# Trainium2 case: the convolution layer's first projection in plain f32 products from the loaded panels, one output tile a panel, with the depthwise convolution tile by tile

## The reference

```
u = rms_norm(h, norm_mix_pre)              # h: 272 x 2048
u = u @ w_in + b_in                        # w_in: 2048 x 4096
a, g = split(u, 2)
u = a * sigmoid(g)
u = causal depthwise convolution of u, 31 taps, + b_dw
u = silu(layer_norm(u, ln_g, ln_b))
u = u @ w_out + b_out
```

## Time and profile before

| quantity | before |
|---|---|
| median of three runs | 3382.66 us (3377.47 to 3384.52) |
| span of the profiled execution, first to last instruction | 3380.4 us |
| TensorE matmul busy | 2816.1 us (83%) |
| VectorE busy | 1935.4 us (57%) |
| ScalarE busy | 949.7 us (28%) |
| GpSimd busy | 944.8 us (28%) |
| mean granted TensorE clock | 0.937 |

### The profile page before, as it was taken

The page is one execution under the profiler, slowest core; times in us unless marked ns, Lnnn a source line. Parts: engine busy times, 40 slices in busy tenths (PEclk is TensorE's granted clock), DMA queues, the critical chain, the costliest instruction groups (busy, mean ns, idle before and its releaser), DMA issues.

```text
span 3380.4 us, 39590 instructions
## 1 busy us (share of the span) xinstructions
PE 2816.1 (83%) x14622; PEld 2102.8 (62%) x14622; DVE 1935.4 (57%) x2548; ACT 949.7 (28%) x1197; POOL 944.8 (28%) x621
## 2 busy tenths in 40 slices
PE   6766397999999997989999997777777787777777
PEld 6766276999999996979999794333333333332233
DVE  4999845555555555385444455555555555655553
ACT  5222235444444444334333342111111111111110
POOL 5777000000000000030000004554545554546452
PEclk9888698999999998899999999989999999899999
DMA  5322043555555553433455547999999999999998
GB/s 215 108 96 105 19 174 112 186 186 186 186 186 186 186 185 113 149 125 142 175 181 195 189 150 298 408 405 411 412 414 411 413 411 412 410 408 409 406 413 339
DMA packets 117532, 855.07 MB, mean 253 GB/s; under 512 B 13104, under 2 KB 13104, under 8 KB 13248
## 3 DMA queue, kind: packets, MB, share of 16 engines
q0 software_dynamic: 74656, 543.27, 39.2%
q1 hardware_dynamic: 42800, 310.85, 25.8%
HBM read 851.97 MB, written 2.10 MB: 253 GB/s over the span
## 4 chain that ended last, share of the span: by engine, by line
PE 44%; DMA 18%; DVE 18%; issue 11%; POOL 5%; ACT 3%; DVEq 0%; POOLq 0%; SPq 0%; ACTq 0%
DMA s_u<-in_expert_u,s_expert 18%; PE bank L1390 14%; PE bank L1392 14%; PE bank L1391 14%; DVE s_u L1319 6%; POOL s_u L466 2%; POOL s_v L473 2%; DVE s_cacc L946 2%; DVE s_w_lo L875 1%; DVE s_yrow L1039 1%; PE bank L1669 1%; DVE s_qrs L1077 1%; ACT s_w_hi L498 1%; POOL s_w_lo L408 1%; ACT s_xs L504 0%
## 5 line engine op out<-in xcount | busy, mean ns | idle before, releaser
L1669 PE MATMUL bank<-s_v,s_diag 128*128 128x512 f32 x2048 | 996.8, 638 | 308.7 <-ACT s_diag L838 178.6
L1390 PE MATMUL bank<-s_a_hi,s_w_hi 128*128 128x256 f32 (+1 forms) x3072 | 883.8, 288 | 104.5 <-POOL s_w_lo L408 80.5
L875 DVE TENSOR_TENSOR s_w_lo<-s_raw,s_w_hi 128x2048 fp32r<-128x2048 f32 x260 | 597.2, 2297 | 647.7 <-ACT s_w_hi L498 647.3
L1669 PEld LDWEIGHTS bank<-s_v,s_diag 128*128 128x128 f32 x2048 | 399.8, 203 | 905.6 <-issue 723.5
L1391 PE MATMUL bank<-s_a_lo,s_w_hi 128*128 128x256 f32 (+1 forms) x3072 | 880.7, 287 | 0.0
L1392 PE MATMUL bank<-s_a_hi,s_w_lo 128*128 128x256 f32 (+1 forms) x3072 | 880.2, 287 | 0.0
L1319 DVE CUSTOM_DVE_ANT_0 s_u<-s_u,s_xn 128x2048 f32<-128x2048 f32 x256 | 583.2, 2292 | 499.6 <-DMA s_u<-in_expert_u,s_expert 497.4
L498 ACT ACTIVATE s_w_hi<-s_raw 128x2048 fp32r<-128x2048 f32 x259 | 496.2, 1916 | 653.0 <-PE bank L1392 652.9
L1390 PEld LDWEIGHTS bank<-s_a_hi,s_w_hi 128*128 128x128 f32 x3072 | 593.7, 193 | 112.6 <-POOL s_w_lo L408 83.9
L1392 PEld LDWEIGHTS bank<-s_a_hi,s_w_lo 128*128 128x128 f32 x3072 | 593.8, 193 | 0.0
L1391 PEld LDWEIGHTS bank<-s_a_lo,s_w_hi 128*128 128x128 f32 x3072 | 590.5, 192 | 1.4 <-issue 1.0
(11 more groups left out here) (264 smaller groups left out, 2169.6 us busy)
## 6 DMA issues: line engine op xcount, KB each, us to landing
s_raw<-in_stream SPq DMA_DIRECT2D x292, 1024.0 KB, 4.8
s_u<-in_expert_u,s_expert POOLq DMA_INDIRECT x256, 15.3
s_v<-in_expert_v,s_expert POOLq DMA_INDIRECT x256, 16.4
s_xres<-in_x SPq DMA_DIRECT2D x2, 1024.0 KB, 6.6
out<-s_out_row SPq DMA_DIRECT2D x2, 1024.0 KB, 6.8
s_bout_row<-in_b_out POOLq DMA_DIRECT2D x1, 1024.0 KB, 8.9
s_gmix_row<-in_g_mix_post POOLq DMA_DIRECT2D x1, 1024.0 KB, 12.4
s_gffn_row<-in_g_ffn_post POOLq DMA_DIRECT2D x1, 1024.0 KB, 16.8
```

What stands on the lines that cost most here:

```text
L875: dve.tensor_tensor(w_lo[s % 2][:, :], raw[s][:, :], w_hi[s % 2][:, :].bitcast(f32), ALU.subtract)\
L1390: pe.matmul(dst, left[0], right[0], start=start, stop=False)
L1669: ins = pe.matmul(bank[4 * t + c][:, :], diag[s % NDIAG][:, :], v_slot[s % NV][:, c * 512:(c + 1) * 512], start=False, stop=False)
```

## The change

* **Weights.** The panels of the first projection are laid out anew (`laid_out`): a panel now holds all 16 input tiles for one output tile; for each pair of output tiles (`a` j, `g` j) there are two panels. There are still 32 panels of 1 MB.
* **Products.** TensorE multiplies straight from `s_raw` with unsplit f32 activations `s_a_f` (a new name for the room of `a_hi` and `a_lo`), 16 matmuls of 272 columns a panel into bank c, 512 matmuls of type f32 in place of 1536 of type f32r. ScalarE's split and GpSimd's subtraction of this stage are gone, and so are the semaphores `hi_half` and `conv_split`.
* **Convolution.** One tile at a time. Even taps add into `cacc[:, 0]`, odd taps into `cacc[:, 1]`, and a last tensor_tensor adds the two sums into `s_cvo`. Taps 0 and 1 are tensor_scalar instructions. ScalarE's sigmoid and VectorE's `glu` also go by single tiles.
* **Prologue.** A root on a constant loads ScalarE's table at the start. ScalarE scales the first 128 tokens and the meta tokens, VectorE the other 128. The eight banks are emptied once: three by ScalarE (`ACT_BANKS`), five by VectorE (`DVE_BANKS`, one instruction a bank), and the meta tokens by one VectorE instruction.
* **Behind.** The layer norm's sum waits for 15 tiles, then for the sixteenth (before 14 and 16). The split of the next projection's first panel follows the stage as before.

The core of the diff:

```diff
+ACT_BANKS = ((0, 3), (1, 1), (1, 3))
+DVE_BANKS = ((0, 0), (0, 1), (0, 2), (1, 0), (1, 2))
...
+    a_f = place("s_a_f", [128, KT, L], S - 2 * ((KT * L * 4 + 63) // 64 * 64))
...
-            with n.rounds(pool, "norm0"):
-                pass
-            with n.rounds(pool, "w_in", 4):
-                for c in range(8):
-                    s = c % 4
-                    for ready, key, half in ((hi_half, "hi_half", slice(0, 1024)), (hi_ready, "hi", slice(1024, 2048))):
-                        pool.wait_ge(ready, n.after(key, c if key == "hi" else c + 1))
-                        ins = pool.tensor_tensor(w_lo[s % 2][:, half], raw[s][:, half], w_hi[s % 2][:, half].bitcast(f32),
-                                                 ALU.subtract)
-                    ins.then_inc(conv_split, 1)
...
+                act.activation(stat[:, 7:8], stat[:, 7:8], ACT.Sqrt)
...
-                for t in range(TT):
-                    act.activation(xs0[:, t, :], xres[:, t, :], ACT.Copy, scale=stat[:, 4 + t:5 + t])\
-                        .then_inc(xs_ready, 1)
+                act.activation(xs0[:, 0, :], xres[:, 0, :], ACT.Copy, scale=stat[:, 4:5]).then_inc(xs_ready, 1)
                 act.activation(meta_sb[:, :], meta_sb[:, :], ACT.Copy, scale=stat[0:META, 6:7]).then_inc(xs_ready, 1)
-                act.wait_ge(raw_loaded[0], 16)
-                act.activation(w_hi[0][:, 0:1024], raw[0][:, 0:1024], ACT.Copy).then_inc(hi_half, 1)
-                act.activation(w_hi[0][:, 1024:], raw[0][:, 1024:], ACT.Copy).then_inc(hi_ready, 1)
                 act.wait_ge(cols_loaded, 16)
-                transposed_hi("g_mix", META)
-                act.wait_ge(panel_used, n.after("used", 1))
-                for k in range(KT):
-                    ins = act.activation(a_hi[:, k, 0:META], bank[0][:, k * META:(k + 1) * META], ACT.Copy,
-                                         scale=col("g_mix", k))
-                ins.then_inc(evac_hi, 1)
+                for t, b in ACT_BANKS:
+                    act.wait_ge(bank_full[4 * t + b], n.after(f"full{4 * t + b}", 1))
+                    for q in range(4):
+                        k = 4 * b + q
+                        ins = act.activation(a_f[:, k, META + t * 128:META + (t + 1) * 128],
+                                             bank[4 * t + b][:, q * 128:(q + 1) * 128], ACT.Copy, scale=col("g_mix", k))
+                    ins.then_inc(bank_empty[4 * t + b], 1)
 
 
             with n.rounds(act, "w_in", 4) as i:
-                for c in range(8):
-                    split_hi(c, halves=True)
-                    if c % 4 < 3:
-                        continue
-                    j = c // 4 * 2
-
-                    act.wait_ge(bank_empty[j + 1], n.after(f"empty{j + 1}", 0))
-                    act.wait_ge(bank_full[4 + j], n.after(f"full{4 + j}", 1))
-                    act.activation(sig[:, j, :], bank[4 + j][:, 0:L], ACT.Sigmoid,
-                                   bias=cols[:, bass.ds(i * 4 + (COL["b_g"] + j), 1)]).then_inc(bank_empty[4 + j], 1)
-                    j += 1
-                    act.wait_ge(panel_used, n.after("used", c + 1))
-                    act.activation(sig[:, j, :], bank[4 + j][:, 0:L], ACT.Sigmoid,
-                                   bias=cols[:, bass.ds(i * 4 + (COL["b_g"] + j), 1)]).then_inc(bank_empty[4 + j], 1)
+                for j in range(4):
+
+                    wait(act, bank_empty[2 * j], n.after(f"empty{2 * j}", 0))
+                    act.wait_ge(panel_used, n.after("used", 2 * j + 2))
+                    act.activation(sig[:, j, :], bank[2 * j + 1][:, 0:L], ACT.Sigmoid,
+                                   bias=cols[:, bass.ds(i * 4 + (COL["b_g"] + j), 1)]).then_inc(bank_empty[2 * j + 1], 1)
+            split_hi(-1)
...
+                dve.wait_ge(rstd_ready, n.after("rstd", 1))
+                dve.tensor_scalar(xs0[:, 1, :], xres[:, 1, :], stat[:, 5:6], None, ALU.mult).then_inc(xs_late_ready, 1)
                 dve.wait_ge(cols_loaded, 16)
-                transposed_lo("g_mix", META)
-                dve.wait_ge(evac_hi, n.after("evac", 9))
-                for k in range(KT):
-                    ins = dve.scalar_tensor_tensor(a_lo[:, k, 0:META], bank[0][:, k * META:(k + 1) * META], col("g_mix", k),
-                                                   a_hi[:, k, 0:META].bitcast(f32), ALU.mult, ALU.subtract)
-                ins.then_inc(bank_empty[0], 1)
+                for t, b in DVE_BANKS:
+                    dve.wait_ge(bank_full[4 * t + b], n.after(f"full{4 * t + b}", 1))
+                    gains = cols[:, COL["g_mix"] + 4 * b:COL["g_mix"] + 4 * b + 4].unsqueeze(2).to_broadcast([128, 4, 128])
+                    dve.tensor_tensor(a_f[:, 4 * b:4 * b + 4, META + t * 128:META + (t + 1) * 128], four_tiles(4 * t + b), gains,
+                                      ALU.mult).then_inc(bank_empty[4 * t + b], 1)
+                dve.wait_ge(panel_used, n.after("used", 1))
+                gains = cols[:, COL["g_mix"]:COL["g_mix"] + KT].unsqueeze(2).to_broadcast([128, KT, META])
+                dve.tensor_tensor(a_f[:, :, 0:META], bank[0][:, 0:KT * META].rearrange("p (k m) -> p k m", k=KT), gains,
+                                  ALU.mult).then_inc(bank_empty[0], 1)
                 link(dve.memset(cvg[:, :, 0:TAPS - 1], 0.0))
 
-            def glu(i, half):
-
-                for j in (2 * half, 2 * half + 1):
-                    if j % 2 == 0:
-                        dve.wait_ge(bank_full[j], n.after(f"full{j}", 1))
-                    else:
-                        dve.wait_ge(panel_used, n.after("used", 4 * half + 2))
-                    dve.wait_ge(bank_empty[4 + j], n.after(f"empty{4 + j}", 1))
-                    dve.scalar_tensor_tensor(cvg[:, j, TAPS - 1:], bank[j][:, 0:L],
-                                             cols[:, bass.ds(i * 4 + (COL["b_a"] + j), 1)], sig[:, j, :],
-                                             ALU.add, ALU.mult).then_inc(bank_empty[j], 1)
-
-            def conv(i, half):
-
+            def glu(i, j):
+
+                dve.wait_ge(panel_used, n.after("used", 2 * j + 2))
+                dve.wait_ge(bank_empty[2 * j + 1], n.after(f"empty{2 * j + 1}", 1))
+                dve.scalar_tensor_tensor(cvg[:, j, TAPS - 1:], bank[2 * j][:, 0:L],
+                                         cols[:, bass.ds(i * 4 + (COL["b_a"] + j), 1)], sig[:, j, :],
+                                         ALU.add, ALU.mult).then_inc(bank_empty[2 * j], 1)
+
+            def conv(i, j):
+
+
+                dve.wait_ge(bank_empty[2 * j], n.after(f"empty{2 * j}", 1))
                 for tap in range(TAPS):
-                    for j in (2 * half, 2 * half + 1):
-                        w = cols[:, bass.ds(i * (4 * TAPS) + (COL["w_dw"] + j * TAPS + tap), 1)]
-                        u = cvg[:, j, META + tap:META + tap + T]
-                        if tap == 0:
-                            dve.wait_ge(bank_empty[j], n.after(f"empty{j}", 1))
-                            b = cols[:, bass.ds(i * 4 + (COL["b_dw"] + j), 1)]
-                            step(dve.tensor_scalar(cacc[:, j, :], u, w, b, ALU.mult, ALU.add))
-                            continue
-                        settled(1)
-                        if tap < TAPS - 1:
-                            step(dve.scalar_tensor_tensor(cacc[:, j, :], u, w, cacc[:, j, :], ALU.mult, ALU.add))
-                        else:
-                            step(dve.scalar_tensor_tensor(
-                                cvo[:, bass.ds(i * 4 + j, 1), :].rearrange("p a t -> p (a t)"), u, w, cacc[:, j, :],
-                                ALU.mult, ALU.add))
+                    w = cols[:, bass.ds(i * (4 * TAPS) + (COL["w_dw"] + j * TAPS + tap), 1)]
+                    u = cvg[:, j, META + tap:META + tap + T]
+                    acc = cacc[:, tap % 2, :]
+                    if tap == 0:
+                        step(dve.tensor_scalar(acc, u, w, cols[:, bass.ds(i * 4 + (COL["b_dw"] + j), 1)], ALU.mult, ALU.add))
+                        continue
+                    if tap == 1:
+                        step(dve.tensor_scalar(acc, u, w, None, ALU.mult))
+                        continue
+                    settled(1)
+                    step(dve.scalar_tensor_tensor(acc, u, w, acc, ALU.mult, ALU.add))
                 settled()
-                dve.memset(stat[:, 7:8], 1.0).then_inc(conv_ready, 1)
+                dve.tensor_tensor(cvo[:, bass.ds(i * 4 + j, 1), :].rearrange("p a t -> p (a t)"), cacc[:, 0, :], cacc[:, 1, :],
+                                  ALU.add).then_inc(conv_ready, 1)
+                dve.wait_ge(conv_ready, n.after("conv", j + 1))
 
 
             with n.rounds(dve, "w_in", 4, dve_step=4 * TAPS) as i:
-                for half in range(2):
-                    glu(i, half)
-                    conv(i, half)
-            split_lo(-1)
+                for j in range(4):
+                    glu(i, j)
+                    conv(i, j)
```

(34 more changed lines are left out.)

34 lines of the change are left out of this document (12 added, 22 removed).

## The result

The changed kernel takes 3268.28 us (median of 4 runs, 3265.09 to 3273.84); the kernel before, run beside it, 3382.51 us. The ratio is 0.9668 [0.9655, 0.9682]: 114 us less, where 110 were forecast (3272.5 us, range 3262 to 3296). A second set of 5 runs gave 3267.96 us, ratio 0.9676 [0.9663, 0.9689]. The profiled execution spans 3272.1 us, 108.3 less than before.

The account below looks back on a forecast made before the run. VectorE's convolution, slowed by GpSimd's subtractions, was taken as the stage's bound, TensorE afterwards: 22.1 + 1.4 + 236 = 259.5, then the end at 273.7; 110.5 us off 3380.4 gives 3270, plus 2.3 to the median 3272.5 us, range 3262 to 3296.

Parts of the forecast that it names:

- 1. Prologue: Before the first projection: first product at 22.1 us in place of 34.78, 12.7 us gained, bounds 11 and 14.
- the bound from the two-input row: Prologue: VectorE scales its half of the tokens in at most 2.29 us, as L875 does for 2048 elements.
- 2. Products: First projection on TensorE: 512 plain f32 matmuls, 0.229 us a record, 236 us, bounds 233 and 240; last ends at 259.5.
- The half clock at the start: First products on TensorE: 1.2 GHz for a while costs 2.6 us, or 0 if absent; 1.4 taken.
- 3. Convolution: VectorE's tiles: 13.4 us each, 214 us for sixteen, under TensorE's 236; VectorE waits about 1.3 us a tile.
- rival B: Convolution: a tile costs 15.5 us, so VectorE is the bound; 3286 us, chance 0.07.
- two sums by turns keep the distance of two tiles by turns: Convolution: dependent taps stay equally far apart, so no gain or loss in the pace was priced.
- 4. End: After the last product: sigmoid, some 0.8 us, and one 13.4 us tile; split at 273.7 in place of 384.24, 110.5 us gained.
- The range's own terms: Whole kernel: prologue 1.5 each way, products -3 and +4, half clock -1.4 and +1.3, norm 0 to -3, scatter 4 us.
- Rival C: Convolution: the slow pace was not GpSimd's doing, so no gain; 3382 us, chance 0.04.
- 0.58 us a tap: Convolution before the change: 58 taps in 33.6 us with GpSimd busy, read as a slow pace against 0.40 without it.
- Rivals A and D: First projection's products: A, granted clock wavers, 3314 us, chance 0.10; D, half clock through the stage, 3509 us, chance 0.03.

Follow-up runs that it names:

- The written-out form: Changed kernel with 8 of 16 products a panel, VectorE's four rounds written out in place of a loop: 3238.35 us, 0.9582.
- The last experiment: Changed kernel, all products, with VectorE's four rounds written out and 40 idle TensorE products at the end of the stage: 3264.77 us, 0.966.

## Why the prediction was right

*1. Prologue: right.* First product at 22.36, forecast 22.1. VectorE scaled its half in 1.29 us, where the bound from the two-input row was 2.29; ScalarE's 2.00 us set the start of the transposes.

*2. Products: right.* 0.229 us a record, 234.9 us in all, for 236. The half clock at the start was absent in one profile and cost 1.7 us in another; the 1.4 taken between them was a mean of two cases, not a state of its own. Last product at 257.3, forecast 259.5. The swing of the clock that the Trainium skill (TensorE: Matmul & The Clock Gate, A second HAM failure mode: psum-queue depth-cycling) describes did not come: 1.00 over 235.3 us while the products went round eight banks, but also without the short idling that its rule speaks of. For plain f32 the Trainium skill (FP8 and Floating Point Precision, TensorE Precision Notes) has four passes; the estimate from them was 232 us, measured 234.9, so the trace agrees.

*3. Convolution: TensorE is the bound, but by less than forecast.* The tile's 13.4 us were short of the 13.7 to 13.9 measured, and nothing was put down for the start of a round, 3.2 us at each of three. The written-out form, at 13.18 us a tile, shows that 0.7 us of a tile are the loop form's work with registers. The round starts could have been read in the trace of before, whose waits from 20 to 420 us have them: the longest of these six are 3.16, 3.22 and 3.20 us, one at the start of each of rounds 2 to 4.

```profile
DVE s_cvg L929 <- issue: 15.2, 6, 3.2
```

The 29 taps themselves took 11.75 us, forecast 11.6. VectorE therefore waited 3.7 us in the stage for its sigmoids after the first, not 1.3 us a tile. The forecast's number held only because VectorE stayed just below TensorE: rival B (15.5 us a tile) needed 2 us more on 13.4, and the real distance was 58.4 against 58.7 us a round of four. That was luck: the size of the margin was wrong, and its sign held. The last experiment shows the forecast's own picture, 1.4 us in the mean before a gated input, once those terms are gone. The sentence that two sums by turns keep the distance of two tiles by turns is borne out by the pace, 0.40 us; the price of not keeping it is 107 us.

*4. End: right.* Last product to split 14.6 us (271.94 - 257.3), forecast 14.2 (273.7 - 259.5). The split moved by 112.3 us, the forecast said 110.5. The profiled span shrank by 108.3 only, and the medians by 114; the 4 us between the one execution and the other come behind this stage, within the scatter of the runs. The range's own terms, added up, reach down to 3260 and not 3262; nothing hangs on it.

*The cause of the slow taps.* Rival C is out: GpSimd's subtractions alone bring back 79 us of the gain, and the new convolution without the new products gains nothing. The forecast named the right cause, from evidence that was weaker than it looked. It took 11 taps at 0.40 us in a gap of GpSimd for the proof, but before the change 26 taps ran at the same 0.40 us while GpSimd's subtraction of 12.33 us was under way. The "0.58 us a tap" was no pace at all, but a mean of many taps of 0.48 us, 0.40 us apart, and a few held for 2.55. Of the 112 us, with the new products in place the new order of the convolution is worth 12.4 us, and the new scaling is not told from the scatter; the rest comes from the plain products, which silence GpSimd and, together with the shorter prologue, start 12.4 us earlier. How much each of these brings was not measured apart; giving GpSimd's load back moved the split by 83 of the 112 us. Rivals A and D didn't come: the clock never fell once the stage was under way.

## What to carry to other kernels

Before handing work to GpSimd, read the shortest, median and longest duration of VectorE's instruction beside it: a median that stays (481 ns) with a maximum of 2655 ns means that single instructions are held for the length of GpSimd's, and the mean hides it. To be sure, give the load back alone, as above. Here a fifth more work for TensorE (235 us of products for 192 at full clock) was the cheaper price. When two engines come close to balance, small terms decide which is the bound, so count the start of each round and what the loop form adds to each tile, look for both in the trace of before, and write a short loop out if they matter. In a chain of dependent VectorE instructions, put an independent one between each two: here 0.40 us from start to start in place of 0.63.

## What was not expected of the hardware

- VectorE's taps and GpSimd's subtractions took turns by whole instructions: 34 taps of 464 lasted 2.55 us instead of 0.48, and a subtraction (median 2.54 us) that came while taps followed without a break took up to 13.8 us.
- A GpSimd multiplication with one input, 1024 columns, took longer than a subtraction with two (2.79 us in the median against 1.95, both beside the taps), and cost VectorE half as much (40 us against 79 for 64 of them): a tap beside it lasted 1.25 us, not 2.08.
- The loop form, with waited values and addresses in registers, cost VectorE about 0.7 us a tile of 33 instructions, and the start of a round 3.2 to 3.5 us, in two of the profiles also 4.3, 4.9 and 6.0; neither has another engine as releaser.
- The lower clock at the first products came and went with the same prologue and the same gap of 0.8 us ahead of the products: mean granted clock 0.79 from 22 to 30 us in the second profile of the changed kernel, 1.00 in the first. Over the twelve profiles with this stage, seven have 0.79 and five 1.00. One thing goes with it: the 32 transposes ahead of the products took 5.3 to 5.8 us in the five and 5.9 to 6.6 us in the seven. What lies behind that stays open.
